# Gate products of a gated linear recurrence: two 64x128 row tiles in place of block-diagonal 128x128 products

## The chip, the cores and the metric

One core of one Trainium2 chip runs the whole kernel. The metric is the device time of one execution in microseconds (us), measured from run to run; the median of 3 runs of the kernel before is 1262.2 us (1261.91 to 1263.3).

## What is computed

A two-layer mixer block works on 256 latent and 256 context tokens of 2048 features, in fp32. Each layer makes one large input projection, splits it into three branches (a convolution module, a bidirectional gated recurrence, windowed attention), gates each and sends them through an output projection. The change concerns the recurrence's two gates, `r` and `i`. They are products with small square matrices: 512 channels in 8 blocks of 64, each block with its own 64x64 matrix.

```python
D_LRU, LRU_BLOCKS, LRU_BLOCK, LRU_C = 512, 8, 64, 8.0

def rglru_scan(x, h0, conv_w, conv_b, w_r, b_r, w_i, b_i, lam):
    xc = depthwise_conv(x, conv_w, conv_b, (LRU_CONV_WIDTH - 1, 0))
    xb = xc.reshape(xc.shape[:-1] + (LRU_BLOCKS, LRU_BLOCK))
    r = jax.nn.sigmoid(jnp.einsum("blhi,hij->blhj", xb, w_r).reshape(xc.shape) + b_r)
    i = jax.nn.sigmoid(jnp.einsum("blhi,hij->blhj", xb, w_i).reshape(xc.shape) + b_i)
    log_a = -LRU_C * r.astype(jnp.float32) * jax.nn.softplus(-lam.astype(jnp.float32))
    a = jnp.exp(log_a)
    bx = jnp.sqrt(-jnp.expm1(2.0 * log_a)) * (i * xc).astype(jnp.float32)
    ...  # h[t] = a[t] * h[t-1] + bx[t]
```

This is done for two directions `d`, in both layers, for 4 channel tiles `t` of 128 channels (two blocks of 64 each), over 512 token positions.

## The kernel before

**Blocks.** The work is a row of 56 blocks a layer; a block is one 128-column tile of a projection, 16 contraction tiles deep. Its weights arrive by DMA (SyncE issues) into one of three `raw` buffers. ScalarE rounds half a block into `w_hi` (`hi`, L1006), VectorE computes the rest into `w_lo` (`lo`, L1354), and TensorE makes three products for each contraction tile (L789 to L791: high by high, high weight by low activations, low weight by high activations). `w_hi` and `w_lo` have four slots, each for one half-block, called a unit here: `hi(u)` waits until TensorE is done with unit `u - 4`. Units are numbered through: in layer 1 block `b` has units 114 + 2b and 115 + 2b. A product is 512 tokens wide in layer 0 and for the recurrence's, key and value blocks of layer 1, and 256 in the others of layer 1 (blocks 4 to 11, and from 16 on).

**Order.** Every engine has its instructions in a fixed order, written as one loop over the blocks with tables that say at which block a side task stands. In block `b` ScalarE does both roundings for block `b + 2`, the evacuation of `b`, then side tasks; VectorE the two `lo` of block `b + 2`, with the recurrence's scan between them, the evacuation, then side tasks. Semaphores join the engines; each engine takes its own queue strictly in order.

**The recurrence.** Four side tasks for each channel tile `t`, at the blocks of these tables (layer 0, layer 1):

```python
LRU_TAPS = [[7, 8, 10, 12], [4, 6, 9, 11]]
LRU_MM = [[8, 10, 12, 14], [6, 9, 11, 13]]
LRU_ROOT = [[9, 11, 13, 15], [7, 10, 12, 14]]
LRU_SCAN = [[10, 12, 14, 16], [8, 11, 13, 15]]
```

- `taps` (L1576, L1580), VectorE: the short convolution, into `Y`, read back through `lru_x(t, d)`.
- `lru_mm` (L816), TensorE: for each direction `d` and gate `g`, one fp32 product of a 128x128 weight tile with 512 columns, into bank `2 * d + g` of `psS` (`psum_scores`). The weight tile of `bd` has two 64x64 gate matrices on its diagonal and zeros elsewhere. It waits for the taps, and for `t > 0` until ScalarE has read the banks of `t - 1`. In layer 0 the `ada` products follow it (L629, column tiles of 32 columns, four of them side by side), in layer 1 the next block.
- `lru_act` (L1134 to L1149), ScalarE: two tanh for each direction out of the banks, then exp, tanh and square. For `t > 0` it waits for `lru_h` of `t - 1`, the sum of both directions' states (L1610, VectorE), since it overwrites `T`.
- `lru_sqrt` (L1154) on ScalarE and `lru_v` (L1586, L1589), `lru_scan` (L1596 to L1610) on VectorE finish the tile.

VectorE's queue in layer 1 also holds the long convolution (L1623), in portions of a fixed number of taps a block.

**The gate weights.** `gate_weights(l)` on SyncE makes four transfers into `bd`, whose space serves as a weight buffer before and as attention's high parts after; POOL fills it with zeros first (L608 in layer 0, L605 in layer 1).

Of the kernel before, what the change touches and what calls it, by code (L numbers as in the profile page):

```python
# [20 lines left out]
ACT = mybir.ActivationFunctionType  # L21
# [16 lines left out]
CT = 4  # L38
# [205 lines left out]
def program(nc, io, known):  # L244
    ctx = ExitStack()
    with ctx:
# [21 lines left out]
        T, TR = both("T", [P, 8, TOK])  # L268
# [89 lines left out]
        def last_of(n):  # L358

            return max(i for i in range(opened) if SLOT[i] == n)  # L360
# [4 lines left out]
        def used(i):  # L365

            item = STREAM[i]
            if item[0] == "w":
                return C.at("lo", unit(0, item[1], 1))
            if item[0] == "chunk":  # L370
                return C.at("lo", chunk_unit(item[1], False))
            if item[0] == "open":
                return C.at("lo", quarter_unit(item[1], SIDE // 2 - 1))
            if item[0] == "pw":
                return C.at("pw_mm", item[1], CT - 1)
            if item[0] == "gate":
                return C.at("gate_acc", item[1])
            return C.at(item[0] + "_mm", *item[1:])
# [119 lines left out]
        def _(sp):  # L498
# [5 lines left out]

            def gate_weights(l):

                sp.wait_ge(*C.at("bd_zero", l))
                for g in range(2):
                    for j in range(2):
                        sp.dma_start(bd[64 * j:64 * j + 64, g, :, 64 * j:64 * j + 64],  # L510
                                     io["lru_w"][l, g, j]).then_inc(*C.up("bd_in", l, g, j, by=16))

            def residual(m):
# [84 lines left out]
        @block.gpsimd  # L598
        def _(pool):
            nc.gpsimd.memset(cstat[:, :], 0.0).then_inc(*C.up("cstat_zero"))  # L600
            nc.gpsimd.memset(eps[:, :], EPS).then_inc(*C.up("eps_set"))
            for l in range(LAYERS):
                if l:
                    pool.wait_ge(*C.at("pv", l - 1, max(groups(l - 1))))
                    nc.gpsimd.memset(bd[:, :, :, :], 0.0).then_inc(*C.up("bd_zero", l))  # L605
                else:
                    pool.wait_ge(*used(last_of(BD_SLOT)))
                    nc.gpsimd.memset(bd[:, :, :, :], 0.0).then_inc(*C.up("bd_zero", l))  # L608
                    for slot_of_q in Q_SLOTS:
                        pool.wait_ge(*used(last_of(slot_of_q)))  # L610
                nc.gpsimd.memset(lrux[:, :, :, :], 0.0).then_inc(*C.up("lrux_zero", l))
                if l == 0:
                    pool.wait_ge(*used(last_of(GLU_SLOT)))
                    nc.gpsimd.memset(glu[:, :, :, :], 0.0).then_inc(*C.up("glu_zero"))
# [3 lines left out]
        def _(pe):  # L618
# [186 lines left out]
            def lru_mm(l, t):  # L805

                pe.wait_ge(*C.at("taps", l, t, 1))
                if t == 0:
                    pe.wait_ge(*C.at("bd_in", l, 1, 1))
                    for b in range(2, min(6, OPEN[l])):  # L810
                        pe.wait_ge(*C.at("evac_act", l * NB + b))
                else:
                    pe.wait_ge(*C.at("lru_tanh", l, t - 1, 1))
                for d in range(2):
                    for g in range(2):
                        last = mm(psS[:, 2 * d + g, :], bd[:, g, d * CT + t, :], lru_x(t, d), start=True, stop=True)  # L816
                last.then_inc(*C.up("lru_mm", l, t))

            def scores(l, s):
# [177 lines left out]
        def _(act):  # L997
# [129 lines left out]
            def lru_act(l, t):  # L1127

                act.wait_ge(*C.at("lru_mm", l, t))
                if t:  # L1130
                    act.wait_ge(*C.at("lru_h", l, t - 1))
                for d in range(2):
                    c = (l * 2 + d) * CT + t
                    fn(T[:, 4 * d + 1, :], psS[:, 2 * d, :], ACT.Tanh, scale=0.5, bias=hbr[:, c:c + 1]  # L1134
                       ).then_inc(*C.up("lru_tanh", l, t, d, "r"))
                    fn(T[:, 4 * d + 2, :], psS[:, 2 * d + 1, :], ACT.Tanh, scale=0.5, bias=hbi[:, c:c + 1]
                       ).then_inc(*C.up("lru_tanh", l, t, d))
                for d in range(2):
                    c = (l * 2 + d) * CT + t
                    act.wait_ge(*C.ago("lru_tanh", 2 - 2 * d + 1))  # L1140
                    fn(T[:, 4 * d + 3, :], T[:, 4 * d + 1, :], ACT.Exp, scale=s4n[:, c:c + 1], bias=s4n[:, c:c + 1]
                       ).then_inc(*C.up("lru_a", l, t, d))
                for d in range(2):
                    c = (l * 2 + d) * CT + t
                    act.wait_ge(*C.ago("lru_a", 1 - d))
                    fn(T[:, 4 * d + 1, :], T[:, 4 * d + 1, :], ACT.Tanh, scale=s4[:, c:c + 1], bias=s4[:, c:c + 1]
                       ).then_inc(*C.up("lru_t", l, t, d))
                for d in range(2):
                    fn(q[:, d, :], T[:, 4 * d + 3, :], ACT.Square).then_inc(*C.up("lru_a2", l, t, d))  # L1149
# [743 lines left out]
```

## Time and profile before

| what | value |
|---|---|
| median of 3 runs | 1262.2 us (1261.91 to 1263.3) |
| profiled execution, from its first to its last instruction (span) | 1262.1 us |
| TensorE (PE) busy | 1225.4 us, 97% |
| VectorE (DVE) busy | 794.3 us, 63% |
| ScalarE (ACT) busy | 543.5 us, 43% |
| POOL busy | 9.8 us, 1% |
| mean granted TensorE clock | 0.993 |

The profiled execution's own time is its span, 1262.1 us; what may lie around the span isn't shown apart. Busy time is the union of an engine's instructions. An fp32 product appears as two matmul records and two weight loads; the products of rounded parts as one each. The column PEclk gives the share of full clock that was granted.

### The profile page before, as it was taken

The numbers are of one execution on the slowest core, as the hardware profiler recorded it, in microseconds if no ns is written. First come the engines' busy times: TensorE is split into PE (matmuls) and PEld (weight loads), VectorE is DVE, ScalarE is ACT, GpSimd is POOL, SyncE is SP. The second block draws the span as 40 slices with busy tenths as digits, with TensorE's granted clock in tenths as the row PEclk, the third lists the DMA queues.
The fourth block names the chain that finished last, engine by engine and source line by source line (L and its number), as shares of the span: only waits on it lengthen the run. The fifth ranks groups of instructions, "written<-read, shape, count | busy, mean of one in ns | idle before, by whom it ended". The sixth has DMA issues, their size and how long they took to land.

```text
span 1262.1 us, 16910 instructions
## 1 busy us (share of the span) xinstructions
PE 1225.4 (97%) x6838; PEld 975.6 (77%) x6838; DVE 794.3 (63%) x1252; ACT 543.5 (43%) x857; POOL 9.8 (1%) x11
## 2 busy tenths in 40 slices
PE   3999999999999999999999999999999999999996
PEld 1555776666777777776778888989888988899995
DVE  5444556766756667763465555696799977656554
ACT  5222445542223433355342222355775455575542
POOL 0000100000000000000000000000000000000000
PEclk9899999999999999999999999999999999999998
DMA  9999756555764444333446666433332544325542
GB/s 335 350 348 348 228 189 232 221 201 204 266 246 167 142 142 166 129 111 142 153 165 231 221 225 225 151 134 133 136 107 101 196 144 150 119 103 205 189 167 67
DMA packets 80894, 236.36 MB, mean 187 GB/s; under 512 B 9392, under 2 KB 54192, under 8 KB 59440
## 3 DMA queue, kind: packets, MB, share of 16 engines
q1 hardware_dynamic: 80816, 235.27, 52.5%
q8 instruction: 54, 0.88, 0.3%
q14 instruction: 24, 0.20, 0.1%
HBM read 230.54 MB, written 2.10 MB: 184 GB/s over the span
## 4 chain that ended last, share of the span: by engine, by line
PE 94%; DMA 2%; DVE 2%; SPq 1%; ACT 1%; issue 0%; DVEq 0%; ACTq 0%
PE psum_block L789 23%; PE psum_block L790 22%; PE psum_block L791 22%; PE psum_ada L629 4%; PE psum_ada L666 2%; PE psum_scores L816 2%; PE psum_scores L717 1%; PE psum_scores L866 1%; PE psum_scores L853 1%; PE psum_scores L719 1%; PE psum_scores L718 1%; PE psum_scores L886 1%; SPq L578 1%; DMA glu<-in_w_ada 1%; DMA raw<-in_w_ada 1%; PE psum_block L913 1%
## 5 line engine op out<-in xcount | busy, mean ns | idle before, releaser
L789 PE MATMUL psum_block<-h_hi,w_hi 128*128 128x256 f32 (+1 forms) x1648 | 562.1, 341 | 0.3 <-DVE h_lo L1346 0.3
L790 PE MATMUL psum_block<-h_lo,w_hi 128*128 128x256 f32 (+1 forms) x1648 | 553.4, 336 | 0.0
L791 PE MATMUL psum_block<-h_hi,w_lo 128*128 128x256 f32 (+1 forms) x1648 | 553.2, 336 | 0.0
L1354 DVE TENSOR_TENSOR w_lo<-raw,w_hi 128x1024 fp32r<-128x1024 f32 x210 | 254.7, 1223 | 332.7 <-ACT w_hi L1006 332.4
L1006 ACT ACTIVATE w_hi<-raw 128x1024 fp32r<-128x1024 f32 x210 | 220.3, 1057 | 444.0 <-PE psum_block L791 409.5
L789 PEld LDWEIGHTS psum_block<-h_hi,w_hi 128*128 128x128 f32 x1648 | 312.7, 190 | 61.8 <-issue 26.9
L790 PEld LDWEIGHTS psum_block<-h_lo,w_hi 128*128 128x128 f32 x1648 | 312.9, 190 | 32.7 <-issue 1.9
L791 PEld LDWEIGHTS psum_block<-h_hi,w_lo 128*128 128x128 f32 x1648 | 312.8, 190 | 32.6
L1623 DVE SCALAR_TENSOR_TENSOR Y<-glu,small,Y 128x512 f32<-128x512 f32 (+1 forms) x240 | 130.4, 612 | 0.0
L1163 ACT ACTIVATE T<-psum_scores,stats 128x512 f32<-128x512 f32 (+1 forms) x48 | 29.0, 616 | 46.5 <-DVE stats L1671 46.5
L629 PE MATMUL psum_ada<-raw,cstat 128*32 128x512 f32 x384 | 47.8, 600 | 0.0
L1060 ACT ACTIVATE h_hi<-T,ada 128x256 fp32r<-128x256 f32 x64 | 28.5, 501 | 44.2 <-DVE T L1418 44.2
L1388 DVE SCALAR_TENSOR_TENSOR kv<-raw,cstat,kv 128x2048 f32<-128x2048 f32 x15 | 35.2, 2345 | 1.1 <-DMA raw<-in_w_ada 1.0
L1366 DVE TENSOR_REDUCE tiny<-psum_ada 128x4 f32<-128x32 f32 x16 | 2.3, 186 | 50.0 <-PE psum_ada L674 50.0
L1169 ACT ACTIVATE T<-T,stats 128x512 f32<-128x512 f32 (+1 forms) x48 | 27.4, 641 | 13.6 <-DVE stats L1681 13.6
L1580 DVE SCALAR_TENSOR_TENSOR Y<-qreg,small,Y 128x512 f32<-128x512 f32 x48 | 32.5, 747 | 0.0
L1354 DVE TENSOR_TENSOR w_lo<-qreg,w_hi 128x1024 fp32r<-128x1024 f32 (+1 forms) x16 | 17.5, 1092 | 19.5 <-ACT w_hi L1006 18.4
L1035 ACT ACTIVATE T<-Y 128x512 f32<-128x512 f32 (+1 forms) x46 | 24.3, 544 | 10.8 <-DVE Y L1546 8.6
L816 PE MATMUL psum_scores<-Y,bd 128*128 128x512 f32 x64 | 28.8, 592 | 0.0
L1424 DVE SCALAR_TENSOR_TENSOR h_lo<-T,ada,h_hi 128x256 fp32r<-128x256 f32 x64 | 27.8, 480 | 1.3 <-ACT h_hi L1060 1.3
L1418 DVE SCALAR_TENSOR_TENSOR T<-Y,A,tbuf 128x256 f32<-128x256 f32 x64 | 27.6, 481 | 0.6
L717 PE MATMUL psum_scores<-h_hi,w_hi 128*128 128x512 f32 x64 | 27.9, 436 | 0.0
(212 smaller groups left out, 1193.3 us busy)
## 6 DMA issues: line engine op xcount, KB each, us to landing
raw<-in_w_blocks SPq DMA_DIRECT2D x105, 1024.0 KB, 4.9
raw<-in_w_ada SPq DMA_DIRECT2D x81, 1024.0 KB, 6.8
qreg<-in_w_blocks SPq DMA_DIRECT2D x8, 896.0 KB, 11.5
glu<-in_w_ada SPq DMA_DIRECT2D x5, 1024.0 KB, 11.6
kv<-in_w_ada SPq DMA_DIRECT2D x5, 1024.0 KB, 11.9
bd<-in_w_ada SPq DMA_DIRECT2D x5, 1024.0 KB, 11.9
Y<-in_xT SPq DMA_DIRECT2D x8, 512.0 KB, 8.1
T<-in_xT SPq DMA_DIRECT2D x16, 256.0 KB, 5.2
```

The costliest lines, as they stand in the source:

```text
L629: last = mm(psA[32 * j:32 * j + 32, :], cstat[:, c_at(k):c_at(k) + 32], w[:, j * TOK:(j + 1) * TOK], start=(k == 0), stop=(k == DT - 1), t ...
L717: mm(ps, hi, hh[:, k, :], start=(k == 0), stop=False)
L789: mm(ps[:, cols], hi, hh[:, k, t], start=(at == 0), stop=False)
L790: mm(ps[:, cols], hi, hl[:, k, t], start=False, stop=False)
L791: last = mm(ps[:, cols], lo, hh[:, k, t], start=False, stop=(at == DT - 1))
L816: last = mm(psS[:, 2 * d + g, :], bd[:, g, d * CT + t, :], lru_x(t, d), start=True, stop=True)
L1006: fn(wh[:, u % 4, 0:cols.stop - cols.start], raw_of(item)[:, cols], ACT.Copy).then_inc(*C.up("hi", u))
L1163: fn(T[:, g, k0:TOK], psS[:, g, k0:TOK], ACT.Exp, scale=SCALE, bias=st[:, 1, g:g + 1], accum_out=st[:, 2, g:g + 1]).then_inc(*C.up("att_ex ...
L1354: V.tensor_tensor(wl[:, u % 4, 0:n], raw_of(item)[:, cols], wh[:, u % 4, 0:n].bitcast(F32), ALU.subtract).then_inc(*C.up("lo", u))
L1388: stt(acc, w, cstat[:, c_at(k):c_at(k) + 1], acc, ALU.mult, ALU.add).then_inc(*C.up("gate_acc", k))
L1580: stt(out, x, lcw[:, c, k:k + 1], out, ALU.mult, ALU.add).then_inc(*C.up("taps", l, t, d))
L1623: stt(out, x, dwh[:, c:c + 1], out, ALU.mult, ALU.add).then_inc(*C.up("conv", l, t, k))
```

## The change

The two gates of a direction were two products, one for each gate, each over all 128 rows with a block-diagonal weight tile. Now they are two products over 64 rows each: product `j` takes the rows of block `j` of the tile, and its weight tile of 64 rows and 128 columns holds both gates' matrices side by side. `tile_position=(64 * j, 0)` puts it on the upper or the lower half of the array. For `j = 0` gate `r` comes out on partitions 0 to 63 and `i` on 64 to 127, for `j = 1` the other way round. So `r` of the whole tile lies on its own partitions, over two banks; `i` lies crosswise, and the tanh that reads it writes it to the other half. Each of ScalarE's tanh over 128 partitions becomes two over 64. Nothing in `bd` has to be zero any longer, so both fills are gone, and the transfers of the gate weights wait for what the fills waited for.

```diff
             def gate_weights(l):
 
-                sp.wait_ge(*C.at("bd_zero", l))
+                sp.wait_ge(*(C.at("pv", l - 1, max(groups(l - 1))) if l else used(last_of(BD_SLOT))))
                 for g in range(2):
                     for j in range(2):
-                        sp.dma_start(bd[64 * j:64 * j + 64, g, :, 64 * j:64 * j + 64],
+                        side = 64 * (g ^ j)
+                        sp.dma_start(bd[64 * j:64 * j + 64, 0, :, side:side + 64],
                                      io["lru_w"][l, g, j]).then_inc(*C.up("bd_in", l, g, j, by=16))
...
                 if l:
                     pool.wait_ge(*C.at("pv", l - 1, max(groups(l - 1))))
-                    nc.gpsimd.memset(bd[:, :, :, :], 0.0).then_inc(*C.up("bd_zero", l))
                 else:
-                    pool.wait_ge(*used(last_of(BD_SLOT)))
-                    nc.gpsimd.memset(bd[:, :, :, :], 0.0).then_inc(*C.up("bd_zero", l))
                     for slot_of_q in Q_SLOTS:
...
                 for d in range(2):
-                    for g in range(2):
-                        last = mm(psS[:, 2 * d + g, :], bd[:, g, d * CT + t, :], lru_x(t, d), start=True, stop=True)
+                    for j in range(2):
+                        rows = slice(64 * j, 64 * j + 64)
+                        last = mm(psS[:, 2 * d + j, :], bd[rows, 0, d * CT + t, :], lru_x(t, d)[rows, :, :],
+                                  start=True, stop=True, tile_position=(64 * j, 0))
                 last.then_inc(*C.up("lru_mm", l, t))
...
                 for d in range(2):
                     c = (l * 2 + d) * CT + t
-                    fn(T[:, 4 * d + 1, :], psS[:, 2 * d, :], ACT.Tanh, scale=0.5, bias=hbr[:, c:c + 1]
-                       ).then_inc(*C.up("lru_tanh", l, t, d, "r"))
-                    fn(T[:, 4 * d + 2, :], psS[:, 2 * d + 1, :], ACT.Tanh, scale=0.5, bias=hbi[:, c:c + 1]
-                       ).then_inc(*C.up("lru_tanh", l, t, d))
+                    for j in range(2):
+                        rows = slice(64 * j, 64 * j + 64)
+                        fn(T[rows, 4 * d + 1, :], psS[rows, 2 * d + j, :], ACT.Tanh, scale=0.5, bias=hbr[rows, c:c + 1]
+                           ).then_inc(*C.up("lru_tanh", l, t, d, "r"))
+                    for j in range(2):
+                        rows, other = slice(64 * j, 64 * j + 64), slice(64 - 64 * j, 128 - 64 * j)
+                        fn(T[rows, 4 * d + 2, :], psS[other, 2 * d + j, :], ACT.Tanh, scale=0.5, bias=hbi[rows, c:c + 1]
+                           ).then_inc(*C.up("lru_tanh", l, t, d))
                 for d in range(2):
                     c = (l * 2 + d) * CT + t
-                    act.wait_ge(*C.ago("lru_tanh", 2 - 2 * d + 1))
+                    act.wait_ge(*C.at("lru_tanh", l, t, d, "r"))
```

On ScalarE, around the gates of the third channel tile of layer 1 (block 11), this stood in its queue before. `T` and `psum_scores` are the gates' buffer and banks, L1006 is the rounding of the weights of block 14.

```order
L1134 ACT_TABLE_LOAD
L1134 ACTIVATE T<-psum_scores,small 128x512
L1136 ACTIVATE T<-psum_scores,small 128x512
L1134 ACTIVATE T<-psum_scores,small 128x512
L1136 ACTIVATE T<-psum_scores,small 128x512
L1141 ACTIVATE T<-T,der 128x512 x2
L1146 ACTIVATE T<-T,der 128x512 x2
L1149 ACTIVATE qreg<-T 128x512 x2
L1006 ACTIVATE w_hi<-raw 128x1024 x2
```

And this stands there now.

```order
L1136 ACT_TABLE_LOAD
L1136 ACTIVATE T<-psum_scores,small 64x512 x2
L1140 ACTIVATE T<-psum_scores,small 64x512 x2
L1136 ACTIVATE T<-psum_scores,small 64x512 x2
L1140 ACTIVATE T<-psum_scores,small 64x512 x2
L1145 ACTIVATE T<-T,der 128x512 x2
L1150 ACTIVATE T<-T,der 128x512 x2
L1153 ACTIVATE qreg<-T 128x512 x2
L1006 ACTIVATE w_hi<-raw 128x1024 x2
```

Four instructions over 128 partitions have become eight over 64, all of them ahead of the rounding. The same holds for the other seven calls. On TensorE four products stand at the same place of the queue as before, and VectorE's queue is the same.

On POOL these fills stood in the queue before.

```order
L608 MEMSET bd 128x2048
L611 MEMSET qreg 128x2096
L614 MEMSET glu 128x2288
L605 MEMSET bd 128x2048
L611 MEMSET qreg 128x2096
```

And these stand there now.

```order
L609 MEMSET qreg 128x2096
L612 MEMSET glu 128x2288
L609 MEMSET qreg 128x2096
```

The two fills of `bd` are gone, and the others follow in the same order.

## Rows read from the trace of the kernel before

**Rows 1.** The page's chain of work that ended last, by engine.

```profile
PE 94%; DMA 2%; DVE 2%; SPq 1%; ACT 1%; issue 0%; DVEq 0%; ACTq 0%
```

**Rows 2.** Timeline of TensorE, layer 0: start, us, engine, line, operation, tiles, count.

```profile
209.95 0.39 PE L790 MATMUL psum_block<-h_lo,w_hi 128*128 128x512 f32 x1
210.18 0.39 PE L791 MATMUL psum_block<-h_hi,w_lo 128*128 128x512 f32 x1
210.40 3.60 PE L816 MATMUL psum_scores<-Y,bd 128*128 128x512 f32 x8
213.93 0.64 PE L629 MATMUL psum_ada<-raw,cstat 128*32 128x512 f32 x4
```

**Rows 3.** Timeline of TensorE at column tiles: the first 0.1 us, then whole.

```profile
351.28 0.64 PE L629 MATMUL psum_ada<-raw,cstat 128*32 128x512 f32 x4
...
350.96 0.39 PE L791 MATMUL psum_block<-h_hi,w_lo 128*128 128x512 f32 x1
351.28 1.93 PE L629 MATMUL psum_ada<-raw,cstat 128*32 128x512 f32 x16
353.13 0.50 PE L789 MATMUL psum_block<-h_hi,w_hi 128*128 128x512 f32 x1
353.47 0.40 PE L790 MATMUL psum_block<-h_lo,w_hi 128*128 128x512 f32 x1
```

**Rows 4.** Stretches: us, then busy PE, PEld, DVE, ACT, POOL, clock, DMA share, GB/s.

```profile
180.00:280.00 100.00, 100.00 (x463) 67.67 (x462) 65.73 (x94) 54.66 (x72) 0.00 (x0) 1.00 0.56 217
...
904.00:940.00 36.00, 36.00 (x205) 29.70 (x205) 33.36 (x51) 26.47 (x37) 0.00 (x0) 1.00 0.33 118
940.00:985.00 45.00, 45.00 (x242) 37.97 (x240) 43.98 (x83) 25.57 (x34) 0.00 (x0) 1.00 0.29 100
```

**Rows 5.** Timeline of ScalarE, layer 1; in brackets idle time before, and its releaser.

```profile
890.23 0.69 ACT L1134 ACTIVATE T<-psum_scores,small 128x512 f32<-128x512 f32 x1 [2.05 <-PE psum_scores L816]
...
917.16 2.00 ACT L1006 ACTIVATE w_hi<-raw 128x1024 fp32r<-128x1024 f32 x2
...
931.12 1.28 ACT L1134 ACT_TABLE_LOAD   x1 [5.49 <-DVE Y L1610]
932.42 0.69 ACT L1134 ACTIVATE T<-psum_scores,small 128x512 f32<-128x512 f32 x1
...
934.71 1.53 ACT L1141 ACTIVATE T<-T,der 128x512 f32<-128x512 f32 x2
...
938.58 2.01 ACT L1006 ACTIVATE w_hi<-raw 128x1024 fp32r<-128x1024 f32 x2
...
961.89 2.00 ACT L1006 ACTIVATE w_hi<-raw 128x1024 fp32r<-128x1024 f32 x2
```

**Rows 6.** Timeline of VectorE, layer 1: the low halves of weights that the text names.

```profile
904.28 1.23 DVE L1354 TENSOR_TENSOR w_lo<-raw,w_hi 128x1024 fp32r<-128x1024 f32 x1 [1.70 <-ACT w_hi L1006]
...
919.51 2.36 DVE L1354 TENSOR_TENSOR w_lo<-raw,w_hi 128x1024 fp32r<-128x1024 f32 x2
...
939.67 2.36 DVE L1354 TENSOR_TENSOR w_lo<-raw,w_hi 128x1024 fp32r<-128x1024 f32 x2 [2.29 <-ACT w_hi L1006]
...
962.98 1.23 DVE L1354 TENSOR_TENSOR w_lo<-raw,w_hi 128x1024 fp32r<-128x1024 f32 x1 [0.74 <-ACT w_hi L1006]
...
973.62 1.22 DVE L1354 TENSOR_TENSOR w_lo<-raw,w_hi 128x1024 fp32r<-128x1024 f32 x1
...
983.87 2.35 DVE L1354 TENSOR_TENSOR w_lo<-raw,w_hi 128x1024 fp32r<-128x1024 f32 x2
```

**Rows 7.** Timeline of TensorE, layer 1: first products of units 146 and 150.

```profile
973.05 0.36 PE L789 MATMUL psum_block<-h_hi,w_hi 128*128 128x256 f32 x1
...
985.15 0.39 PE L789 MATMUL psum_block<-h_hi,w_hi 128*128 128x256 f32 x1
```

**Rows 8.** Stretches near the start, TensorE alone: us, busy, granted clock, DMA share, GB/s.

```profile
45.00:48.00 3.00, 0.94 (x6) 1.00 1.09 348
...
49.00:52.00 3.00, 3.00 (x11) 0.50 1.09 349
```

## Prediction

> **What bounds the kernel now.** I read the chain of waits first: 94% of it is TensorE [rows 1], so what leaves TensorE's queue leaves the time, as long as nobody else is late. So the question of each stretch is who would be late next. The gate products stand in two stretches: four calls of layer 0 from 180 to 280 us, four of layer 1 from 886 to 951 us. The table by stretch [rows 4] tells them apart. From 180 to 280 us TensorE is busy all the time, VectorE for 66 of 100 us and ScalarE for 55. From 904 to 940 us VectorE is busy for 33.4 of 36 us, and from 940 to 985 us for 44.0 of 45. There TensorE is busy too, but VectorE has nothing left to give: the two run neck and neck, and the timeline of VectorE [rows 6] shows what its few idle moments wait for. TensorE's first product of unit 150 (a unit is half a block's weights; this one is the first half of block 18) starts at 985.15 us [rows 7], just as VectorE ends that unit's low half at 985.1 [rows 6]: the one place of the stretch where TensorE waits.
>
> **TensorE, the gate products themselves.** One call (one channel tile, both directions) is 4 products, each recorded as two matmuls: 8 records in 3.60 us [rows 2], so each record holds the array for 0.43 us; the next work starts 3.53 us after the first record. After a product of the same kind of array there is no gap: L790, L791 and L816 follow each other at 0.22 to 0.23 us [rows 2]. The changed call has 4 products again, in two pairs on the upper and the lower 64 rows. No row tile is in the trace. The nearest rows are the column tiles of the ada products: four of them start within hundredths of a us, as x4 with 0.64 us together [rows 3], and two calls, 16 records, take 1.93 us where one after the other would take 16 x 0.43 = 6.9. So four tiles go at once, and their second records follow 0.43 later. I take the same for two row tiles: 4 slots of 0.43 in place of 8. Ends: nothing is gained (8 slots), or all (4 slots); the column tiles are the same engine, type and width, so I take 4.
>
> The Trainium skill ("TensorE: Matmul & The Clock Gate", Part 3, what overlaps) says that matmuls start and end in program order and never overtake. By that rule, with a product's two records side by side in the queue, the pairs would shift by a slot and 5 slots be needed; the rows of the column tiles speak against it or for another order of the records, and the case is a rival below. The Trainium skill's same part gives 3.07x for four row tiles, so that two tiles may fall short of 2x as well; an estimate of 1.5x from it would be 2.3 us a call in place of 1.7.
>
> A change of the array's split costs something. Going into column tiles: L791 at 350.96, L629 at 351.28, 0.32 where 0.23 is usual, so 0.09 [rows 3]. Coming back: the 16 records from 351.28 need 4 slots, to 353.02; L789 starts at 353.13 and L790 0.34 later instead of 0.23, together 0.2. In layer 0 each call is followed by ada products, so its exit (213.93, 3.53 after the first record, where 8 slots are 3.43) already pays 0.1 now; the change adds an entry and no exit. A call there: 3.53 now; then 0.09 + 4 x 0.43 + 0.1 = 1.91; gain 1.6. In layer 1 the call goes back to full products: 3.43 now, then 0.09 + 1.73 + 0.2 = 2.0; gain 1.4. Bounds of a switch: 0 and twice this, 0.1 to 0.3 a call.
>
> **ScalarE.** Each call's four tanh over 128 partitions become eight over 64, each still 512 wide. Four take 2.29 us, from 932.42 to 934.71 [rows 5]. No activation over 64 partitions with 512 elements is in the trace. Bounds: half the price each (nothing added), or the full price (2.29 us added a call). I take the full one: a ScalarE row's time follows the elements of a partition. The Trainium skill ("ScalarE: Activation LUTs", What ACT_TABLE_LOAD costs) gives 280 ns + 0.833 ns for each element along a partition, whatever their number of partitions; by it an activation of 512 is an estimate of 707 ns either way and the sum the same. No run here shows it yet.
>
> **Layer 0, four calls.** TensorE leaves 4 x 1.6 = 6.4 us earlier. What covers ScalarE's 9.2 extra us: a weight half is rounded by ScalarE and completed by VectorE up to three halves before its products (24 products of 0.227 us each [rows 2], so 16 us), and both are idle for a third or more of the stretch [rows 4]. So I cost them at nothing; if that cover were gone they would cost up to 2.3 a call. **Gain 6.4**, kept.
>
> **Layer 1, four calls.** Here VectorE's queue is the clock. Follow it.
> - Tile 0: ScalarE starts its tanh at 890.23, when the products are done [rows 5]. Products: 2 slots x 2 earlier less the switch, so it starts 4 x 0.43 - 0.1 = 1.6 earlier and runs 2.3 longer: ends 0.7 later. VectorE then waits for roundings that stand behind it in ScalarE's queue, here and at 904.28 [rows 6]. **VectorE 0.7 later.**
> - Tile 1: ScalarE's tanh must wait for the state sum of tile 0 (VectorE, 0.7 later), so it can't start all of 1.6 earlier but only about 0.8, and hands over 1.5 later than now: the first rounding behind it, begun at 917.16 and done at 918.2, will be done at 919.7. VectorE takes it up at 919.51 now and at 920.2 then [rows 5, 6], so it just fits. **Adds 0**, with 0.5 to spare.
> - Tile 2: ScalarE waits 5.49 us for VectorE's state sum at 931 [rows 5], then does table load, tanh and exp, and only then the rounding at 938.58; VectorE waits 2.29 us for it at 939.67 [rows 6]. The TensorE end plays no part. **Adds 2.3.**
> - Tile 3: the same loop: rounding at 961.89, VectorE waits 0.74 at 962.98. **Adds 2.3.**
> After that VectorE works through without a gap up to 985.1. So unit 150 gets its low half 0.7 + 2.3 + 2.3 = 5.3 us later, and TensorE, which by its own products would arrive 4 x 1.4 = 5.6 earlier, stands and waits. **Loss 5.3**; the 5.6 that the four calls save there are worth nothing.
>
> Where the wait goes: mostly to unit 148. Its low half ends at 974.8 now [rows 6], at 980.1 then. TensorE starts unit 146 at 973.05 now [rows 7]. Four units and some transposes fill the 12.1 us to unit 150, so 148 comes about 6.1 after 146. TensorE would start 146 about 5 earlier (the 5.6, less a short wait on the way), at 968, but waits 1.5 for that unit's low half (962.98 + 1.23 + 5.3), reaches 148 at 975.6 and stands for some 4.5 us, then twice about 2.2 us before units 149 and 150.
>
> **The clock.** Such a standstill may bring down TensorE's clock. At 45 to 48 us TensorE was busy for 0.94 of 3 us, and at 49 to 52 us it was granted 0.50, that is 1.2 of 2.4 GHz, while fully busy [rows 8]. 3 us at half rate are worth 1.5 us of products. Where the fall comes before unit 149 it is hidden in the next wait (cost 0); after unit 150 all of it counts (1.5). Neither end is nearer; I take **0.8**.
>
> **The other parts.** The two POOL memsets of `bd` go. SyncE's gate-weight transfers wait for their releasers directly; they aren't needed until block 8 or 6, so 0. They are the same four transfers of the same size. The other memsets stand behind them in POOL's queue and come up to 2 us earlier, which nobody waits for. Nothing passes another step on SP's queue. VectorE has the same instructions.
>
> **Sum.** -6.4 + 5.3 + 0.8 = -0.3, against the 1262.1 us span of the profiled execution; the median 1262.2 differs from it by 0.1. I forecast 1261.9, with 1259.5 to 1264.5 as this case's own range (clock 0 to 3, switches 0 to double, tile 1's margin used up). What a measurement of this kernel tells from no change is about 0.2%, 2.5 us: 1259.7 to 1264.7.
>
> **Rivals.**
> - The tanh over 64 partitions costs half. Then ScalarE adds nothing, and layer 1's chain moves by tile 0 alone, 1.6 earlier, since VectorE still works without a gap. -6.4 - 1.6 = -8.0: 1254.1. For it: nothing in the trace has 64 partitions. Against: other ScalarE rows follow the width. Chance 0.10. Halfway, about 1258: 0.07.
> - Pairs are offset by a slot (5 slots in place of 4). Each call loses 0.43: layer 0 gains 4.7, tile 0's start is 0.43 later: -0.3 + 1.7 + 0.4 = +1.8: 1263.9, and it decides by how the two records of a product are queued. For it stands the skill's rule on order, against it the x4 row. Chance 0.12.
> - Slower: row tiles don't run at once at all, so the change doesn't do what it says. The place is the 8 calls: 8 slots plus switches, layer 0 +0.1 a call, tile 0 of layer 1 hands over 2.4 later. 0.4 + 2.4 + 4.6 + clock 0.8 = +8.2: 1270.3. Against: the column tiles. It decides from about 7 slots a call on. Chance 0.10.
> - Slower: the clock falls twice or stays down beyond unit 150. At half rate for 6 us after it, 3.0 in place of 0.8: 1264.1, and up to 1266 if it falls again. Chance 0.09.
> The forecast has the remaining 0.52.
>
> **Chances.** Faster: 0.10 + 0.07 and 0.01 of the forecast = 0.18. Slower: 0.10 of the serial case, 0.05 of the clock's, 0.04 of the offset's, 0.03 of the forecast = 0.22. Within 0.2%: 0.60. The range leaves out the half-price tanh and the serial case, together 0.20: 1257.0 to 1266.5.
>
> **What would show it.** The eight gate records of a call within some 2 us, starting in twos; eight tanh rows with a 64-partition form at 0.69 us, and ScalarE's busy time up by 8 x 2.29 = 18 us. Between 180 and 280 us no TensorE idle, and layer 0 over 6 us sooner. In layer 1 the two waits of VectorE for roundings (2.29 and 0.74 us) each grown to 4.6 and 3.0, and TensorE idle for some 10 us between 950 and 985, released by VectorE's low half. I am wrong if TensorE stays busy there, if the records don't start in twos, or if layer 0's stretch shortens by less than 5 us.

## Result: 1271.1 us, slower by 0.8%

| | before | changed |
|---|---|---|
| median of 4 runs, us | 1262.06 (1261.03 to 1263.3) | 1271.13 (1270.79 to 1273.95) |
| ratio, 95% interval | | 1.0078 [1.0065, 1.009] |
| span of the profiled execution, us | 1262.1 | 1272.2 |
| granted clock, mean | 0.993 | 0.987 |

Busy time after: TensorE 1220.9 us, VectorE 794.5, ScalarE 567.6. The forecast was 1261.9 with a range up to 1266.5: the kernel became slower, outside the range. The profiled execution is the longest of the four (1273.95), some 2.8 above the median. So the accounts below, which add up to 10.0 of the 10.1 between the two spans, explain that execution; the measured change is 9.1.

### The profile after, beside the rows of before

The chain of waits by engine. In [rows 1] it was 94% TensorE:

```profile
PE 84%; DVE 6%; ACT 5%; SPq 3%; issue 1%; DMA 1%; DVEq 0%; ACTq 0%
```

**The calls themselves did what was forecast.** The timeline of TensorE at the call in layer 0: its first 0.1 us, then the whole. In [rows 2] it was 3.60 us with `128*128`.

```profile
181.18 0.70 PE L815 MATMUL psum_scores<-Y,bd 64*128 64x512 f32 x2
...
181.18 1.99 PE L815 MATMUL psum_scores<-Y,bd 64*128 64x512 f32 x8
183.10 1.06 PE L627 MATMUL psum_ada<-raw,cstat 128*32 128x512 f32 x8
```

Two records start together, and the next work begins 1.92 us after the first record; 1.91 was forecast. The four calls move the units behind them by 1.51, 1.55, 1.55 and 1.52 us, so unit 32 comes 6.1 us sooner.

**Then layer 0 loses it all.** TensorE and ScalarE at block 15, where before there was no wait (the first two rows are TensorE's, the others ScalarE's in the blocks 14 and 15):

```profile
273.93 0.39 PE L789 MATMUL psum_block<-h_hi,w_lo 128*128 128x512 f32 x1
277.99 1.12 PE L650 MATMUL psum_ada<-rounded,lnr 128*128 128x128 f32 x4 [3.68 <-ACT lnr L1016]
...
267.35 0.60 ACT L1115 ACTIVATE tbuf<-psum_block 128x512 f32<-128x512 f32 x1
267.84 1.37 ACT L1136 ACTIVATE T<-psum_scores,small 64x512 f32<-64x512 f32 x2
269.24 1.39 ACT L1140 ACTIVATE T<-psum_scores,small 64x512 f32<-64x512 f32 x2
270.66 1.39 ACT L1136 ACTIVATE T<-psum_scores,small 64x512 f32<-64x512 f32 x2
272.08 1.39 ACT L1140 ACTIVATE T<-psum_scores,small 64x512 f32<-64x512 f32 x2
273.49 1.52 ACT L1145 ACTIVATE T<-T,der 128x512 f32<-128x512 f32 x2
274.92 1.50 ACT L1150 ACTIVATE T<-T,der 128x512 f32<-128x512 f32 x2
276.33 1.13 ACT L1153 ACTIVATE qreg<-T 128x512 f32<-128x512 f32 x2
277.37 0.57 ACT L1016 ACTIVATE lnr<-psum_ada 128x512 f32<-128x512 f32 x1
```

The adaLN transposes (L650) need the copied rows (`lnr`, L1016), and the copy stands in ScalarE's queue behind the whole gate chain of tile 3: eight half tanh, two exp, two tanh, two squares. The same copy in the kernel before:

```profile
272.90 0.69 ACT L1134 ACTIVATE T<-psum_scores,small 128x512 f32<-128x512 f32 x1 [0.41 <-PE psum_scores L816]
...
279.07 0.59 ACT L1016 ACTIVATE lnr<-psum_ada 128x512 f32<-128x512 f32 x1
```

It ended at 279.66 and TensorE wanted it 0.6 later. Now it ends only 1.7 us sooner, at 277.94, while TensorE is 6.1 us sooner. On top of the wait, the table by stretch shows TensorE at 0.50 of its clock, that is 1.2 of 2.4 GHz, from 277 to 284 us, where before it had 1.00 all along [rows 4]:

```profile
180.00:280.00 100.00, 96.32 (x471) 66.34 (x470) 66.84 (x95) 67.46 (x89) 0.00 (x0) 0.99 0.58 224
904.00:940.00 36.00, 35.70 (x219) 29.94 (x218) 33.55 (x52) 28.71 (x39) 0.00 (x0) 1.00 0.39 144
940.00:985.00 45.00, 40.44 (x193) 33.38 (x191) 34.97 (x68) 33.19 (x44) 0.00 (x0) 0.92 0.22 77
277.10:283.80 6.70, 5.81 (x16) 4.75 (x17) 1.41 (x3) 1.78 (x3) 0.00 (x0) 0.50 0.02 6
```

(The first three answer to [rows 4].) The wait of 3.7 and the slow stretch together move the units from 34 on back by 6.55 (unit 33, which starts early in the slow stretch, by 4.2). Layer 0 ends 0.6 later than before, in place of 6.4 sooner.

**Layer 1 loses 9.4.** VectorE's rows behind the four calls, to be held against [rows 6]:

```profile
900.02 2.36 DVE L1358 TENSOR_TENSOR w_lo<-raw,w_hi 128x1024 fp32r<-128x1024 f32 x2 [5.29 <-ACT w_hi L1006]
...
922.82 2.36 DVE L1358 TENSOR_TENSOR w_lo<-raw,w_hi 128x1024 fp32r<-128x1024 f32 x2 [0.68 <-ACT w_hi L1006]
...
946.35 2.36 DVE L1358 TENSOR_TENSOR w_lo<-raw,w_hi 128x1024 fp32r<-128x1024 f32 x2 [5.66 <-ACT w_hi L1006]
...
973.03 2.36 DVE L1358 TENSOR_TENSOR w_lo<-raw,w_hi 128x1024 fp32r<-128x1024 f32 x2 [4.12 <-ACT w_hi L1006]
```

The waits at the four tiles were 3.42, 0, 2.29 and 0.74 (the first is this row of before):

```profile
897.48 2.36 DVE L1354 TENSOR_TENSOR w_lo<-raw,w_hi 128x1024 fp32r<-128x1024 f32 x2 [3.42 <-ACT w_hi L1006]
```

They grew by 1.87, 0.68, 3.37 and 3.38, together 9.3, and the end of layer 1's stretch moved by 9.4. TensorE only passes it on, standing before the products it can't start (its timeline, the longest of the waits):

```profile
902.86 0.36 PE L787 MATMUL psum_block<-h_hi,w_hi 128*128 128x256 f32 x1 [1.80 <-DVE glu L1526]
...
974.48 1.12 PE L973 MATMUL psum_misc<-rounded,tbuf 128*128 128x128 f32 x4 [3.47 <-ACT tbuf L1109]
...
984.95 0.39 PE L787 MATMUL psum_block<-h_hi,w_hi 128*128 128x256 f32 x1 [1.09 <-DVE w_lo L1358]
...
990.11 0.39 PE L787 MATMUL psum_block<-h_hi,w_hi 128*128 128x256 f32 x1 [2.03 <-DVE w_lo L1358]
...
995.20 0.39 PE L787 MATMUL psum_block<-h_hi,w_hi 128*128 128x256 f32 x1 [0.47 <-DVE w_lo L1358]
```

The last of these is unit 150: 985.15 in [rows 7], 995.20 now.

**Why ScalarE is that late.** Eight half tanh start 0.71 us apart (pairs of 1.39 us, each begun 1.40 to 1.42 behind the last) and take 5.65 to 5.68 until the next step. Four whole ones took 2.29 [rows 5], since each starts 0.57 after the one ahead although it lasts 0.69. A half tanh lasts 0.68 and does not begin before the half tanh ahead of it is over. So a call costs ScalarE 3.4 more, not 2.3.

### The profile page after: what moved, and what is told of

It is laid out like the page before. It is cut to its first block, busy times and chain, and to the rows that moved or that the text cites. A ratio compares the mean times of both kernels' runs of the same rounds, so it can differ in the third digit from the quotient of the medians.

```text
span 1272.2 us, 16940 instructions
## 1 busy us (share of the span) xinstructions
PE 1220.9 (96%) x6838; PEld 974.7 (77%) x6838; DVE 794.5 (62%) x1252; ACT 567.6 (45%) x889; POOL 6.2 (0%) x9
## 4 chain that ended last, share of the span: by engine, by line
PE 84%; DVE 6%; ACT 5%; SPq 3%; issue 1%; DMA 1%; DVEq 0%; ACTq 0%
PE psum_block L787 20%; PE psum_block L788 20%; PE psum_block L789 20%; PE psum_ada L627 3%; SPq L579 2%; PE psum_ada L664 2%; DVE w_lo L1358 1%; PE psum_scores L715 1%; PE psum_scores L866 1%; PE psum_scores L853 1%; PE psum_scores L717 1%; DVE Y L1627 1%; PE psum_scores L716 1%; PE psum_scores L886 1%; ACT T L1140 1%; ACT T L1136 1%
## 5 line engine op out<-in xcount | busy, mean ns | idle before, releaser
L1006 ACT ACTIVATE w_hi<-raw 128x1024 fp32r<-128x1024 f32 x210 | 219.9, 1056 | 426.4 <-PE psum_block L789 397.6
L1403 DVE TENSOR_TENSOR T<-T 128x512 f32<-128x512 f32 (+1 forms) x42 | 25.1, 598 | 2.9 <-ACT T L1035 1.5
```

What stands on the lines that cost most here:

```text
L1006: fn(wh[:, u % 4, 0:cols.stop - cols.start], raw_of(item)[:, cols], ACT.Copy).then_inc(*C.up("hi", u))
```

## The experiments

Theory A: row tiles halve the calls, and what turns that into a loss are the half tanh on ScalarE, through two queues: the copied rows in layer 0, the roundings that VectorE needs in layer 1. Rivals: the row tiles or the single `bd` layout cost something of their own (B), the copy isn't what holds block 15 (C), and others named with the runs.

Besides the time, each run gives the move of the unit marks against before, in its own profiled execution and from its own first unit on: over layer 0 (to unit 60) and over layer 1 (unit 60 to 165). Behind that nothing moves in any of them. The place of the first unit itself varies by 2.8 us from one execution to the next, so that the two columns don't add up exactly to a median.

| kernel | median, us | ratio [95%] | layer 0 | layer 1 |
|---|---|---|---|---|
| the change | 1271.13 | 1.0078 [1.0065, 1.009] | +0.6 | +9.4 |
| e1 whole tanh | 1255.78 | 0.9949 [0.9934, 0.9964] | -5.7 | -1.5 |
| e2 half tanh only | 1279.45 | 1.0131 [1.0116, 1.0146] | +4.6 | +12.6 |
| e3 rows between | 1267.02 | 1.0038 [1.0023, 1.0052] | -5.7 | +9.4 |
| e4 layer 0 only | 1257.76 | 0.9958 [0.9944, 0.9973] | -5.8 | 0.0 |
| e5 by half | 1269.91 | 1.0064 [1.0049, 1.0079] | -1.2 | +8.8 |
| e6 quadrants | 1261.33 | 0.9999 [0.999, 1.0008] | -5.0 | +5.9 |
| e7 filler | 1270.74 | 1.0064 [1.0047, 1.0081] | -2.1 | +11.1 |
| e8 one tile | 1264.42 | 1.0022 [1.0013, 1.0031] | 0.0 | +2.1 |
| e9 early rounding | 1257.71 | 0.9968 [0.9956, 0.9981] | -6.2 | +2.6 |
| e10 e4 and early rounding | 1257.01 | 0.9959 [0.9945, 0.9974] | -5.8 | -0.2 |
| e11 lower, then upper | 1273.39 | 1.0091 [1.0076, 1.0106] | +2.2 | +7.9 |
| e12 layer 1 only | 1271.43 | 1.0076 [1.0061, 1.0091] | 0.0 | +9.4 |

### e1 and e2: one half of the change each

e1 is the change with four whole tanh (half of the partitions then take the other gate's product: a part of the computation is changed). e2 is the kernel before with eight half tanh.

```diff
-                    for j in range(2):
-                        rows = slice(64 * j, 64 * j + 64)
-                        fn(T[rows, 4 * d + 1, :], psS[rows, 2 * d + j, :], ACT.Tanh, ...
+                    fn(T[:, 4 * d + 1, :], psS[:, 2 * d, :], ACT.Tanh, ...
```

> The changed kernel with row tiles, but with four tanh over all 128 partitions a call as before (the two gates are mixed up on half of the partitions: that part of the computation is changed). Theory A: the loss is ScalarE's, whose eight half tanh take 5.7 us a call where four took 2.3; with four the row tiles bring about 5.7 in layer 0 (a wait of some 0.4 us for the ada rows stays) and 1.6 in layer 1: about 1255, no fall of the clock after 60 us. Rival B: row tiles and what they do to TensorE (switches, clock) cost the time: it stays at 1268 or more with the clock falls at 277 and 973 us.

> The kernel before with its full block-diagonal products, but eight tanh over 64 partitions a call. Theory A: 3.4 us more on ScalarE a call; in layer 0 TensorE then waits 2.8 us for the ada rows, with a clock fall some 5 to 6; in layer 1 the tiles hand over 3.4, 2.1, 3.4 and 3.4 later, 12.3: together 1279 to 1284. Rival B: 1262 to 1265, since no row tile is in it. The spacing of the half tanh also tells whether reading crosswise makes them slow: here none does; 0.71 us if it is the 64 partitions, 0.57 if it is the crossing.

Both as theory A has it. Row tiles alone are a gain of 6.5 us, half tanh alone a loss of 17. In e1 the wait for the copied rows shrinks to 0.32, and layer 1 runs up to 5.2 us ahead (1.3 a call, 1.4 forecast) until VectorE's low halves hold it; 1.5 us are left of it:

```profile
274.77 0.33 PE L650 MATMUL psum_ada<-rounded,lnr 128*128 128x128 f32 x1 [0.32 <-ACT lnr L1016]
...
973.06 0.39 PE L787 MATMUL psum_block<-h_hi,w_hi 128*128 128x256 f32 x1 [1.40 <-DVE w_lo L1354]
...
978.15 0.39 PE L787 MATMUL psum_block<-h_hi,w_hi 128*128 128x256 f32 x1 [1.97 <-DVE w_lo L1354]
```

In e2 nothing is read crosswise (a lower half of psum goes to a lower half of `T`), and the halves still follow each other at 0.71:

```profile
271.58 1.40 ACT L1136 ACTIVATE T<-psum_scores,small 64x512 f32<-64x512 f32 x2 [0.41 <-PE psum_scores L816]
273.00 1.39 ACT L1140 ACTIVATE T<-psum_scores,small 64x512 f32<-64x512 f32 x2
```

So crossing from one half of the partitions to the other costs nothing of its own. B falls.

### e3: the copied rows between the tanh

The change, with the copy (`ada_rows`) of block 14 moved from behind the gate chain to between tanh and exp.

```diff
-            def lru_act(l, t):
+            def lru_act(l, t, between=()):
...
+                for a in between:
+                    ada_rows(*a)
```

> The changed kernel, with ScalarE's copy of the ada rows in block 14 moved from behind the whole gate step to between its tanh and its exp. Theory A: TensorE's wait of 3.7 us at 278 us goes, and with it the clock fall there: 6.5 us sooner, about 1264.5, layer 0 ending 6 us sooner than in the kernel before. Rival C: the clock falls there anyway (the row tiles' doing): only 3.7 sooner, about 1267.5.

Layer 0 keeps 5.7 us and layer 1 is untouched (+9.4): 1267.02, beside 1271.13 for the change in a session of its own. C falls: the copy now ends at 273.45, and TensorE waits 0.38 us for something else.

```profile
272.85 0.60 ACT L1016 ACTIVATE lnr<-psum_ada 128x512 f32<-128x512 f32 x1
```

From the traces the move is worth 6.3 us, from the medians 4.1, and the expectation (1264.5) was too low. The profiled execution of the change is a long one, and the starts vary; the size of this step is known to about 2 us.

### e4 and e12: one layer each

e4 has e3's row tiles, half tanh and moved copy in layer 0, and the products, the fill and the tanh of before in layer 1. e12 is the complement, without the moved copy.

```diff
-                for d in range(2):
+                for d in range(2 if l == 0 else 0):
...
+                for d in range(2 if l else 0):
+                    for g in range(2):
+                        last = mm(psS[:, 2 * d + g, :], bd[:, g, d * CT + t, :], lru_x(t, d), start=True, stop=True)
```

> Row tiles and half tanh in layer 0 alone, with the same moved copy; layer 1 with full products, fill and four tanh as before. Theory A: layer 0's 6.1 us are kept and layer 1 costs nothing: 1256, faster than both. If layer 1 loses time by what layer 0 leaves behind (transfers, clock), 1262 or more.

> The complement of e4: row tiles and eight half tanh in layer 1 alone, the full products and the POOL fill in layer 0. If the two layers add up (layer 1's +9.4 of the trace of the change, nothing from layer 0): 1271 to 1273. Rival (layer 1's loss hangs on when it is entered, or on the clock's fall in layer 0): 1266 to 1269.

The layers add up: 1257.76 is 4.5 below its before, 1271.43 is 9.6 above, and the sum of +5.1 is e3's +4.7 within the runs' spread. e4 beats both kernels.

### e8: one tile, to test the account of VectorE

```diff
+                    for rows in (slice(0, 64), slice(64, 128)) if (l, t) == (1, 1) else (slice(0, 128),):
```

> The kernel before with eight half tanh in tile 1 of layer 1 alone. Theory A (ScalarE +3.4 in that tile, about 1.3 of it covered ahead of VectorE's wait for the rounded values): VectorE about 2.1 later from there on, TensorE waits as much behind units 48 and up, 1264.3, and up to 3 more if the clock falls in a wait. Rival (a single tile is covered): 1262.3 as before.

+2.1 in the trace, +2.4 in the medians. In tile 1 of before VectorE had no wait; of ScalarE's 3.4 it felt 2.1, and every later row and unit 150 are 2.1 later:

```profile
919.62 2.36 DVE L1356 TENSOR_TENSOR w_lo<-raw,w_hi 128x1024 fp32r<-128x1024 f32 x2 [2.02 <-ACT w_hi L1006]
...
985.26 0.39 PE L789 MATMUL psum_block<-h_hi,w_hi 128*128 128x256 f32 x1 [1.96 <-DVE w_lo L1356]
```

(This execution's first unit came 2.0 us earlier than that of before, so 985.26 is 2.1 later than the 985.15 of [rows 7].) Three of the ten runs took 1266.7 to 1267.4, at a mean clock of 0.992 beside 0.994 to 0.997 in the others; such a loss is what the expectation allows for a fall of the clock, but none of the three has a trace.

A single late hand-over of ScalarE goes through VectorE to the end of the kernel, less what was spare.

### e7: filler, to test the clock's share in layer 0

```diff
+                if l == 0 and b == max(LRU_MM[0]) + 1:
+                    misc_free(l)
+                    for _ in range(22):
+                        mm(psM[:, 0:3 * P], rounded[:, 0, :], rounded[:, :, :].rearrange("p m k -> p (m k)"), start=True, stop=True)
```

> The change with 22 more products into the scratch bank ahead of the adaLN transposes of block 15, so that TensorE works through the wait for the copied rows; nothing else is moved. Theory A (the wait costs 3.7 us by itself and the fall of the granted clock behind it costs about 3 more): no fall behind 278 us, the end about 3 us sooner, 1268. Rival (the clock falls there whatever TensorE does in the wait): 1271 as in the change.

Half of it. With TensorE at work through the wait, the clock stays at 1.00 there and layer 0 is 2.6 us better. But layer 1 is 1.7 us worse. The clock now falls at 900, behind the same wait of 1.8 us that the change passed at full clock (VectorE's `glu`, at 902.86 there), but unit 149 comes only 0.1 later for it, since VectorE's waits stand in between. The rest, 1.5 us, is a fall at 992, right behind the start of unit 150 and so behind the last wait for VectorE (the last two rows are the first products of the units 150 and 151, which follow each other at 4.48 us in place of 2.96). In the change the last fall ended at 993.8, ahead of unit 150 at 995.20, and was hidden in its wait.

```profile
277.00:281.00 4.00, 4.00 (x20) 3.29 (x19) 1.41 (x3) 0.41 (x1) 0.00 (x0) 1.00 0.01 2
900.10:903.40 3.30, 3.30 (x18) 3.30 (x17) 1.61 (x3) 3.29 (x5) 0.00 (x0) 0.50 0.69 283
992.30:995.50 3.20, 3.20 (x17) 3.20 (x16) 3.06 (x5) 0.00 (x0) 0.00 (x0) 0.50 0.16 41
...
991.22 0.39 PE L787 MATMUL psum_block<-h_hi,w_hi 128*128 128x256 f32 x1 [1.97 <-DVE w_lo L1362]
995.70 0.28 PE L787 MATMUL psum_block<-h_hi,w_hi 128*128 128x256 f32 x1
```

The same happens in the traces of e5, e6 and e9: 1.5 us between the units 150 and 151, by a fall of the clock at 991, 983 and 980 us. The end of e7 is 0.4 us lower in the medians than the change, which can't be told from nothing. e3 passed its 1.81 us wait at full clock, e2 did not (2.00 us, 0.50 behind it). Why a wait of this size is followed by a fall in one execution and not in another stays open.

### e5, e6 and e11: when one tanh overlaps the next

e5 orders the eight of the change by the output's half. e11 is e2 with the four of the lower half first. e6 is e3 with each row tile cut into two 64x64 tiles on the four quadrants, so that r lies whole in one bank and takes whole tanh, and i takes halves.

```diff
# e11
+                for j in range(2):
+                    rows = slice(64 * j, 64 * j + 64)
+                    for d in range(2):
...
# e6
+                            rows, side = slice(64 * j, 64 * j + 64), 64 * (g ^ j)
+                            last = mm(psS[side:side + 64, 2 * d + g, :], bd[rows, 0, d * CT + t, side:side + 64],
+                                      lru_x(t, d)[rows, :, :], start=True, stop=True, tile_position=(64 * j, side))
```

> The change, with the eight half tanh of a call issued in the order of the output's half (both first-half chunks of r, both of i, then the second half's), so that each shares its 64 output partitions with the one before it except once. Theory D (two activations overlap if they write the same 64 partitions): starts 0.575 us apart except once, eight take about 4.7 in place of 5.68, some 4 us less over layer 1 and the wait in layer 0 shorter: 1264 to 1268. Theory E (a 64-partition activation never overlaps the next): starts 0.71 apart as in the change, 1271.

> e2 (the kernel before with eight half tanh) with the four of the lower 64 partitions first, then the four of the upper. Theory D2 (an activation overlaps the one ahead if both read and write the same partitions, as the pairs of e5 show): three starts 0.58 apart, one 0.70, three 0.58, eight take 4.85 in place of 5.66, ScalarE +2.5 a call in place of +3.4: 1273 to 1277. Rival E2 (the pairs of e5 overlap for another reason, such as one function and one line): 0.70 for all, 1279 as e2.

> The change with the copy of the adaLN rows moved as in e3, and the gate products as 64x64 tiles on the four quadrants of the array, so that r's bank holds whole chunks and takes one 128-partition tanh each, while i stays crosswise and takes halves: six tanh a call. If four quadrants work at once, a call stays at 1.9 us and ScalarE's term falls from +3.4 to about +1.7 a call: layer 0 -5.8 as in e3, layer 1 about +3.5 in place of +9.4: 1260 to 1263. If tiles of one row group but different column groups go one after the other, a call is about 3.5 us again: nothing gained in layer 0, 1265 to 1268.

e11's tanh in layer 1:

```profile
891.88 0.68 ACT L1136 ACTIVATE T<-psum_scores,small 64x512 f32<-64x512 f32 x1 [2.05 <-PE psum_scores L816]
892.47 0.67 ACT L1138 ACTIVATE T<-psum_scores,small 64x512 f32<-64x512 f32 x1
893.04 0.67 ACT L1136 ACTIVATE T<-psum_scores,small 64x512 f32<-64x512 f32 x1
893.61 0.67 ACT L1138 ACTIVATE T<-psum_scores,small 64x512 f32<-64x512 f32 x1
894.31 0.68 ACT L1136 ACTIVATE T<-psum_scores,small 64x512 f32<-64x512 f32 x1
894.89 0.67 ACT L1138 ACTIVATE T<-psum_scores,small 64x512 f32<-64x512 f32 x1
```

0.59, 0.57, 0.57, then 0.70 where the partitions change, then 0.58 again. Eight take 4.86, and the time falls from 1279.45 to 1273.39. So it is not 64 partitions as such that forbid the overlap, but the change from one set of partitions to another. In e5 the four pairs that read and write the same partitions overlap (0.59 apart, 1.26 a pair); where only the written ones stay the same (888.34 to 889.04, 0.70), or only the read ones (889.63 to 890.33, 0.70), they don't:

```profile
887.76 1.26 ACT L1136 ACTIVATE T<-psum_scores,small 64x512 f32<-64x512 f32 x2 [0.54 <-PE psum_scores L815]
889.04 1.27 ACT L1140 ACTIVATE T<-psum_scores,small 64x512 f32<-64x512 f32 x2
890.33 1.26 ACT L1136 ACTIVATE T<-psum_scores,small 64x512 f32<-64x512 f32 x2
```

Eight take 5.1, in place of 5.65, and the theory that the written half alone decides falls by these rows. The time, 1269.91, is outside its range (1264 to 1268) and can't be told from the change's by the medians: unit 150 comes 7.3 later than before in place of 9.4, but then the fall of the clock takes its 1.5 (see e7).

e6's rows of the call, TensorE and then ScalarE:

```profile
179.00 0.66 PE L816 MATMUL psum_scores<-Y,bd 64*64 64x512 f32 x4
...
881.60 0.69 ACT L1135 ACTIVATE T<-psum_scores,small 128x512 f32<-128x512 f32 x1 [0.52 <-PE psum_scores L816]
882.32 1.39 ACT L1139 ACTIVATE T<-psum_scores,small 64x512 f32<-64x512 f32 x2
883.74 0.69 ACT L1135 ACTIVATE T<-psum_scores,small 128x512 f32<-128x512 f32 x1
```

Four quadrants start at once and a call stays at 1.9 us. Six tanh take 4.28 us, +2.0 a call: a whole tanh beside a half one doesn't overlap here either (0.72). But it isn't the change from 128 partitions to 64 that forbids it. In the change, the evacuation over 128 partitions (`tbuf`, 267.35, 0.60 long) is followed at 267.84 by the half tanh that reads and writes the partitions 0 to 63, 0.1 us before it ends. What all these rows have in common is the partition at which an activation begins: where reading and writing both begin at the same one as in the activation ahead, the two overlap; in e6 one of them begins at the other half at every step. No row shows a lower half followed by a whole one. Layer 1 loses 5.9 in place of 9.4 (4.4 up to unit 150, and 1.5 by the clock), layer 0 keeps 5.0 (it lost 1.3 more in later waits for adaLN weights from DMA). 1261.33, no difference from before.

### e9 and e10: the roundings ahead of the gate chain

e9 is e3 with e5's order, and in layer 1 both roundings of the next block are moved ahead, behind the tanh and behind the exp. e10 is e4 with the same.

```diff
+                early = [unit(0, (l * NB + LRU_MM[l][t]) + 3, i) for i in range(2)] if l else []
+                if early:
+                    hi(early[0])
```

> Row tiles in both layers with e3's moved copy and e5's order of the tanh, and in layer 1 the two roundings of the block behind each gate call moved ahead: the first between tanh and exp, the second between exp and the last tanh. Theory A (layer 1 loses because VectorE waits for roundings that stand behind the gate chain on ScalarE): VectorE's waits of about 5 us at each tile nearly vanish, TensorE keeps part of the 10.7 us that e1 showed in layer 1; with layer 0's 5.7: 1250 to 1256. Rival (ScalarE's chain from state sum to state sum sets the pace, whatever stands between): VectorE waits for exp and square in place of the rounding, layer 1 stays +5 to +9, 1262 to 1266.

> e4 (row tiles in layer 0 alone) with the same early roundings in layer 1. By theory A TensorE's own products bound layer 1 there, and it waited for nobody: as e4, 1256.5 to 1258. If VectorE's queue did hold it up in places the trace doesn't show: 1252 to 1255. What e9 is below this run is what row tiles are worth in layer 1 once the roundings don't stand behind them.

VectorE's waits at the tiles fall apart into short ones (at tile 2, 5.66 us became these three):

```profile
930.89 1.23 DVE L1365 TENSOR_TENSOR w_lo<-raw,w_hi 128x1024 fp32r<-128x1024 f32 x1 [1.27 <-ACT w_hi L1006]
933.25 1.23 DVE L1365 TENSOR_TENSOR w_lo<-raw,w_hi 128x1024 fp32r<-128x1024 f32 x1 [1.13 <-ACT w_hi L1006]
935.18 1.29 DVE L1597 SCALAR_TENSOR_TENSOR qreg<-qreg,T 128x512 f32<-128x512 f32 x2 [0.71 <-ACT qreg L1160]
```

Layer 1 loses 2.6 where it lost 9.4 in e3: 1.1 up to unit 150 (e5's order alone took 2.1 of the 9.4 away, the moved roundings the rest) and 1.5 by the clock behind it. So theory A's path through the roundings is confirmed by taking it away; the rival falls. But e9 misses its range (1250 to 1256): TensorE is 5.2 ahead at unit 146, as in e1, and has given it all back to waits for VectorE's low halves by unit 150. And e10 and e4, without any row tile in layer 1, are as fast: 1257.0 and 1257.8. Row tiles with half tanh are worth nothing in layer 1, because VectorE has no time left to give there.

## Why the prediction was wrong

**The call, 3.53 to 1.91 us, and its sum.** Right: 1.92, and 6.1 us for the four calls of layer 0 (6.4 forecast), 5.2 for those of layer 1 while nothing holds them (e1; 5.6 forecast). The rivals of five slots and of serial row tiles fell. So did half price and halfway: a half tanh takes what a whole one takes.

**"So I cost them at nothing" (layer 0).** This step failed, by 6.6 us. I named a cover for the weight roundings alone. Not followed was what else stands behind the gate chain in ScalarE's queue: the copied adaLN rows of block 14, for which TensorE had 0.6 us to spare in the trace of before. TensorE 6.1 sooner and ScalarE 3.4 longer made it a wait of 3.7 us. By these figures it would be some 2.6 us even with the tanh at my price (an estimate: 3.7 less the 1.1 a call that I had too little). The clock at 0.50 behind it was the other 2.9.

**ScalarE +2.29 a call.** Mis-sized: +3.4. I took the spacing of whole tanh (0.575), in which 0.12 of each is hidden under the next, for halves that alternate. The Trainium skill ("ScalarE: Activation LUTs", What ACT_TABLE_LOAD costs) says that back-to-back activations overlap by some 93 ns, without a condition. The rows show about that overlap where both activations begin at the same partition (0.12), and none where the first partition read or written changes. The length was right: the Trainium skill's figures there are measured on 128 partitions, and here a half tanh lasts 0.68 us beside 0.69.

**VectorE's chain in layer 1, +0.7, 0, +2.3, +2.3.** The mechanism was right, tile by tile, and e8 confirmed it; by the wrong term it came to 5.3 where 9.3 was measured. With 3.4 in place of 2.29 the same steps give 1.8, 0.6 (tile 1's spare 0.5 is used up), 3.4 and 3.4. The place of TensorE's waits was only partly right: the longest is not before unit 148 (1.1) but 3.5 us at the transposes of a value block (L973), whose evacuation stands in ScalarE's queue behind tile 3's gate chain and two roundings; this one and the 1.8 at 903 weren't forecast.

**The clock, +0.8.** In layer 1 it cost nothing to speak of: it fell at 973 and again at 990, but VectorE set the end, and 9.3 of the 9.4 are VectorE's waits. That the cheap end of my term came out was luck: in e5, e6, e7 and e9 the last fall stood behind unit 150 and cost 1.5 us, the dear end that I had named. The fall that counted came in layer 0, where I expected no wait.

Sum against the trace: layer 0 +0.6 in place of -6.4, layer 1 +9.4 in place of +6.1: +10.0 in place of -0.3. The likeliest way of going wrong, a higher price of the half tanh, was in no rival: the bounds were nothing and the full spacing, and the dear end was taken as the most it could be.

## What to carry to other kernels

When an edit lengthens a step of an engine that looks idle, list everything that stands behind that step in its queue, and for each who waits for it and with how much spare in the trace; the share of idle time says nothing about that. A duration taken from a row of back-to-back instructions is a spacing: it may hold an overlap that the new form doesn't have, so the upper bound is the row's own length at least, not the spacing (here even 0.03 us more: 0.71 apart at a length of 0.68). And a gain of one stage can be kept by changing that stage alone: row tiles in layer 0 with the copy moved (e4) are 4.5 us faster than before, while in layer 1, where VectorE is full, they bring nothing (with whole tanh, e1, 1.5 us).

## What the runs showed of the hardware

- In these rows an activation starts before the end of the one ahead where both begin to read at the same partition and both begin to write at the same one: 0.57 to 0.59 us apart for tanh of 512 elements (128 partitions twice, the same 64 twice), and 0.1 us before the end from 128 partitions to the lower 64 (267.84 in the change). Where the first partition read or written changes, it is 0.70 to 0.72 (the change, e2, e5, e6, e11).
- Row tiles of 64x128, and quadrants of 64x64, run at once as column tiles do: the groups of two or of four records follow each other at 0.41 to 0.53 us, 1.9 us a call in place of 3.5.
- Between the first unit and the last stretch of the kernel, TensorE's clock fell to 1.2 GHz at every wait of 2.0 us and more that the traces show (2.00 in e2 to 3.68 in the change), at some of 1.77 to 1.99 us (1.77 in e9, 1.81 in e7) and not at others (1.81 in e3, 1.99 in e11). When e7 took away the fall at 278 us, one came at 900 us and one behind unit 150, and the time stayed.
